# A state space layer in two halves of channels: the first half's tables, inputs and scan inside the input projection

## The reference: what is computed

```python
u = rmsnorm(x, g_mix[1]) @ w_in_c                # 2048 -> 1024 channels
# 64 groups of 16 channels, 64 complex states each
xr, xi = einsum('btgc,gpc->btgp', u, bb_re), einsum('btgc,gpc->btgp', u, bb_im)
xr[:, 0] += ar * s0_re - ai * s0_im              # the past state enters at the first token
sr, si = complex_scan(ar, ai, xr, xi)            # s[t] = a * s[t-1] + x[t], complex, per state
y = einsum('btgp,gcp->btgc', sr, c_re) - einsum('btgp,gcp->btgc', si, c_im) + d_skip * u
y = gelu(y)
mix = (y @ w_glu_v) * sigmoid(y @ w_glu_g)
```

## Time and profile before

| | us |
|---|---|
| median of 3 runs | 2754.16 |
| lowest and highest | 2751.86, 2755.89 |
| the profiled execution | 2755.66 |
| its span in the profile | 2753.1 |
| TensorE busy | 2707.5 (98%) |
| VectorE busy | 1592.7 (58%) |
| ScalarE busy | 1168.8 (42%) |
| GpSimd busy | 445.2 (16%) |

### The profile page before, as it was taken

How to read it: one execution, slowest core, us unless ns; L and a number is a source line. 1 busy time by engine, 2 the same in 40 slices (tenths; PEclk the granted TensorE clock), 3 DMA queues, 4 the chain that set the end, 5 groups by cost and what they waited for, 6 DMA issues and landing times.

```text
span 2753.1 us, 54151 instructions
## 1 busy us (share of the span) xinstructions
PE 2707.5 (98%) x19993; PEld 2676.2 (97%) x19993; DVE 1592.7 (58%) x2615; ACT 1168.8 (42%) x1514; POOL 445.2 (16%) x535
## 2 busy tenths in 40 slices
PE   8999999999999999999999998999999999999997
PEld 7999999999999999999999997999999999999997
DVE  7556666665554455655556657565554555455554
ACT  5554445434343343435554443544433344334333
POOL 1333333330000000070003561310000000000022
PEclk9999999999999999999999999999999999999998
DMA  6444444555545454444444531545555554555453
GB/s 176 133 132 132 135 144 127 147 150 152 144 141 143 143 145 140 135 141 143 143 133 141 145 94 46 150 142 148 150 145 153 147 151 139 152 154 152 143 145 93
DMA packets 739213, 382.97 MB, mean 139 GB/s; under 512 B 13560, under 2 KB 734756, under 8 KB 739140
## 3 DMA queue, kind: packets, MB, share of 16 engines
q1 hardware_dynamic: 722352, 365.34, 46.4%
q10 hardware_dynamic: 14228, 9.31, 1.1%
q0 software_dynamic: 2560, 7.29, 1.0%
HBM read 373.31 MB, written 8.57 MB: 139 GB/s over the span
## 4 chain that ended last, share of the span: by engine, by line
PE 96%; DVE 2%; ACT 1%; issue 0%; DMA 0%; ACTq 0%; SPq 0%; POOL 0%; POOLq 0%; DVEq 0%
PE banks L1591 31%; PE banks L1592 30%; PE banks L1593 30%; PE banks L1656 1%; PE banks L1974 0%; PE banks L2026 0%; PE banks L1871 0%; DVE wl L1032 0%; DMA xin<-in_x_sample 0%; DVE m L1472 0%; DVE m L1470 0%; PE banks L1961 0%; PE banks L1754 0%; PE banks L1652 0%; PE banks L1752 0%
## 5 line engine op out<-in xcount | busy, mean ns | idle before, releaser
L1032 DVE TENSOR_TENSOR wl<-raw,wh 128x1024 fp32r<-128x1024 f32 x708 | 897.0, 1268 | 802.1 <-ACT wh L486 801.3
L1591 PE MATMUL banks<-h,wh 128*128 128x336 f32 (+2 forms) x3648 | 1157.5, 317 | 3.9 <-DVE wl L1078 2.2
L486 ACT ACTIVATE wh<-raw 128x1024 fp32r<-128x1024 f32 x708 | 748.8, 1058 | 949.6 <-PE banks L1593 932.0
L1592 PE MATMUL banks<-h,wh 128*128 128x336 f32 (+2 forms) x3648 | 1146.4, 314 | 0.0
L1593 PE MATMUL banks<-h,wl 128*128 128x336 f32 (+2 forms) x3648 | 1145.0, 314 | 0.0
L1591 PEld LDWEIGHTS banks<-h,wh 128*128 128x128 f32 x3648 | 686.3, 188 | 11.7 <-issue 7.9
L1592 PEld LDWEIGHTS banks<-h,wh 128*128 128x128 f32 x3648 | 686.2, 188 | 1.7
L1593 PEld LDWEIGHTS banks<-h,wl 128*128 128x128 f32 x3648 | 685.5, 188 | 0.0
L1591 PE MATMUL banks<-act,wh 128*128 128x336 f32 (+2 forms) x1872 | 588.1, 314 | 2.7 <-DVE act L1546 2.1
L1592 PE MATMUL banks<-act,wh 128*128 128x336 f32 (+2 forms) x1872 | 585.9, 313 | 0.0
L1593 PE MATMUL banks<-act,wl 128*128 128x336 f32 (+2 forms) x1872 | 585.6, 313 | 0.0
(11 more groups left out here) (370 smaller groups left out, 1700.0 us busy)
## 6 DMA issues: line engine op xcount, KB each, us to landing
raw<-in_w_up SPq DMA_DIRECT2D x172, 512.0 KB, 3.8
raw<-in_w_gate SPq DMA_DIRECT2D x172, 512.0 KB, 3.8
raw<-in_w_down SPq DMA_DIRECT2D x160, 448.0 KB, 3.6
raw<-in_w_in_e SPq DMA_DIRECT2D x96, 512.0 KB, 3.7
raw<-in_w_out_e SPq DMA_DIRECT2D x32, 512.0 KB, 4.0
raw<-in_w_down SPq DMA_DIRECT2D x32, 512.0 KB, 4.0
raw<-in_w_in_c SPq DMA_DIRECT2D x16, 512.0 KB, 3.7
raw<-in_w_glu_v SPq DMA_DIRECT2D x16, 512.0 KB, 4.0
```

The lines of the kernel that those rows point to most:

```text
L486: sc.activation(wh[:, j % RING, :], raw[:, j % RING, :], ACT.Copy).then_inc(rounded, 1)
L1032: v.tensor_tensor(wl[:, j % RING, :], raw[:, j % RING, :], wh[:, j % RING, :].bitcast(F32), ALU.subtract) \
L1591: pe.matmul(out, whi, hi, start=first and k == 0, stop=False)
L1592: pe.matmul(out, whi, lo, start=False, stop=False)
```

## The change

The state space's 8 chunks are treated as two halves of four. Each of the four tables is made, turned and copied once for either half (`TURNED`: eight half tables, the first four for chunks 0 to 3). `BX`, `BT` and the scan's scratch `m0`, `m1` have half the size; the second half's `BT` lies where the first half's was. The states lie in two tensors, `xsA` and `xsB`. TensorE makes input chunks 0 to 3 in the middle and behind tiles (2, 0) and (2, 1), always in banks 4 to 7; chunk 4 directly behind the projection, chunks 5 to 7 after `K5`. ScalarE takes chunks 0 to 3 at the places of `X_TAKEN`. VectorE scans quarters 0 and 1 behind the splits of tiles (2, 1) to (3, 1) (`SCANNED`), quarters 2 and 3 one by one after the projection. The direct path's table is summed in bank 2, its skip is added behind the split of (3, 3) instead of (3, 2). The third readout table goes to a plain `C3` on GpSimd, and ScalarE spreads both `C3` and `C4` into block form. GpSimd copies past states once per half. ScalarE copies the first half's block ends into `SC`. In the diff, lines that only remove the old form are partly left out.

```diff
-BX_TURNED = [(0, 3), (1, 3), (2, 2), (3, 1)]
-BX_COPIED = [(1, 0), (2, 0), (2, 3), (3, 2)]
+TURNED = {(0, 2): 0, (0, 3): 1, (1, 1): 2, (1, 3): 3, (2, 2): 4, (2, 3): 5, (3, 1): 6, (3, 2): 7}
+FOUR_PAIRS = PAIRS // 2
+SCANNED = {(2, 1): ((0, 1),), (2, 2): ((0, 2), (0, 3)), (3, 0): ((1, 1), (1, 2)), (3, 1): ((1, 3),)}
+X_TAKEN = {(1, 3): (0,), (2, 0): (1, 2), (2, 1): (3,)}
...
+        BT, BX, m0, m1 = union(
+            0, ("BT", [P, 4, STEP, 2, P]), ("BX", [P, 2, 4, P]), ("m0", [P, 2, QUARTER * BLK]), ("m1", [P, 2, QUARTER * BLK]),
+            )
+        xsA, st5 = union(16 * slot_bytes - 4 * NS * 2 * PAIRS - 4 * 2 * FOUR_PAIRS * XW, ("xsA", [P, 2, FOUR_PAIRS, XW]), ("st5", [P, NS, 2, PAIRS]))
+        C3, = union(4 * 4 * STEP * 2 * P, ("C3", [P, 2, PAIRS, C5]))
...
+        SCt, = union(8 * slot_bytes, ("SCt", [P, 2, PAIRS, PCH]))
+        g0, g1 = union(0, ("g0", [P, 2, 3, 4, PAIRS]), ("g1", [P, 2, 3, 4, PAIRS]))
...
-        CT3 = BX.rearrange("p r j n -> p (r j) n").rearrange("p (j r) n -> p j r n", r=2)
...
+        xsB, CT3, CT4, SC, fin5 = union(at_h, ("xsB", [P, 2, FOUR_PAIRS, XW]), ("CT3", [P, 8, 2, P]), ("CT4", [P, 8, 2, P]),
+                                        ("SC", [P, PCH, 2, PAIRS]), ("fin5", [P, 1 + NS, 2, PAIRS]))
+        halves5 = (xsA, xsB)
...
-            src = wide[(j + 1) % 2]
-            dst = xs[:, :, 4 * j:4 * j + 4, :].rearrange("p r q x -> p q r x")
+            src = wide[1 if j < 4 else (j + 1) % 2]
+            dst = halves5[j // 4][:, :, j % 4 * 4:j % 4 * 4 + 4, :].rearrange("p r q x -> p q r x")
...
+                    if (i, j) in TURNED:
+                        k = TURNED[i, j]
+                        for r in range(2):
+                            e.wait_ge(bt_t, 2 * k + r + 1)
+                            sc.activation(BT[:, :, k % STEP, r, :], bank[4 + k % 2 * 2 + r].rearrange("p (j n) -> p j n", j=4),
                                           ACT.Copy).then_inc(bt_c, 1)
+                    for m in X_TAKEN.get((i, j), ()):
+                        e.wait_ge(x5, m + 1)
+                        take_x(lambda to, x: sc.activation(to, x, ACT.Copy), m).then_inc(x5a, 1)
...
-            for j in range(8):
+            for j in range(4, 8):
...
+            for n, (to, src, ready) in enumerate(((CT3, C3, c3_made), (CT4, C4, c4_made))):
+                e.wait_ge(ready, 1)
+                e.wait_ge(ct_zero, n + 1)
+                for g in range(2):
+                    rowsl = slice(g * P5, (g + 1) * P5)
+                    for r in range(2):
+                        ins = sc.activation(to[rowsl, :, r, :].rearrange("p j (q g c) -> p j q g c", q=4, g=2)[:, :, :, g, :],
+                                            src[rowsl, r].rearrange("p (j q) c -> p j q c", q=4), ACT.Copy)
+                ins.then_inc(ct34_made, 1)
+            e.wait_ge(scan5, 2)
+            sc.activation(SC[:, :, :, 0:FOUR_PAIRS].rearrange("p c r q -> p r q c"), xsA[:, :, :, 3 * BLK:3 * BLK + PCH], ACT.Copy).then_inc(sc_a, 1)
...
+            past = lambda x, n: gp.tensor_copy(x[:, :, :, BLK + PCH:2 * BLK],
+                                               st5[:, :, :, n * FOUR_PAIRS:(n + 1) * FOUR_PAIRS].rearrange("p s r q -> p r q s"))
+            past(xsA, 0).then_inc(st_a, 1)
             st.then(gp.memset(BX[:], 0.0))
...
+            half = lambda t: t[:, 0:FOUR_PAIRS]
+            other = lambda t: t[:, FOUR_PAIRS:PAIRS]
+            for n in range(2 * STEP):
+                k, j0 = n % STEP, 4 * (n // STEP)
+                own = slice(4 * j0, 4 * j0 + FOUR_PAIRS)
+                if k == 0:
+                    if n:
+                        e.wait_ge(bx_used, n)
+                    for g in range(2):
+                        rowsl = slice(g * P5, (g + 1) * P5)
+                        for r in range(2):
+                            to = BX[rowsl, r].rearrange("p j (q g c) -> p j q g c", q=4, g=2)[:, :, :, g, :]
+                            ins = gp.tensor_copy(to, B2[rowsl, r, own].rearrange("p (j q) c -> p j q c", q=4))
+                else:
+                    times_power(gp, st, B2, k - 1, 0, half(bp), half(bq), OF_B, j0, j0 + 4)
+                    gp.tensor_tensor(other(bp), B2[:, 1, own], power(k - 1, 1)[:, own], ALU.mult)
+                    st.then(gp.tensor_tensor(other(bq), B2[:, 0, own], power(k - 1, 2)[:, own], ALU.mult))
+                    e.wait_ge(bx_used, n)
+                    into_blocks(gp, half(bp), half(bq), BX[:, 0])
+                    ins = into_blocks(gp, other(bp), other(bq), BX[:, 1])
                 ins.then_inc(bx_made, 1)
-                e.wait_ge(bx_made, k + 1)
+                e.wait_ge(bx_made, n + 1)
...
-            e.wait_ge(bx_used, STEP)
...
+            e.wait_ge(bx_used, 2 * STEP)
+            for r in range(2):
+                for j0 in (0, 4):
+                    own = slice(4 * j0, 4 * j0 + FOUR_PAIRS)
+                    second = sq[:, 0:FOUR_PAIRS * C5].rearrange("p (q c) -> p q c", c=C5)
+                    times_power(gp, st, C0, 2, r, C3[:, r, own], second, OF_C, j0, j0 + 4)
+                    st.then(gp.tensor_tensor(C3[:, r, own], C3[:, r, own], second, ALU.add))
+            gp.memset(sq[:, 0:1], 0.0).then_inc(c3_made, 1)
             e.wait_ge(evac, PH["glu"].group(0, 0) + BANK_CREDIT)
-            gp.tensor_copy(xs[:, :, :, BLK + PCH:2 * BLK], st5.rearrange("p s r q -> p r q s")).then_inc(st_in, 1)
-            gp.memset(CT4[:], 0.0).then_inc(ct4_zero, 1)
+            past(xsB, 1).then_inc(st_in, 1)
+            for to in (CT3, CT4):
+                gp.memset(to[:], 0.0).then_inc(ct_zero, 1)
...
+            def scan_step(u, i):
+                q, xs = slice(u * QUARTER, (u + 1) * QUARTER), halves5[u // 2]
+                own = slice(u % 2 * QUARTER, (u % 2 + 1) * QUARTER)
+                if i == 1:
+                    e.wait_ge(x5a, 2 * u + 2)
+                    e.wait_ge(st_a, 1)
+                n = PCH if i == 1 else PCH + NS
+                prev, cur = (xs[:, :, own, BLK * k:BLK * k + n] for k in (i - 1, i))
+                A0 = AP5[:, 1:2, 3, q].unsqueeze(3).to_broadcast([P, 2, QUARTER, n])
+                A1 = AP5[:, 0::2, 3, q].unsqueeze(3).to_broadcast([P, 2, QUARTER, n])
+                m = lambda t: t[:, :, 0:QUARTER * n].rearrange("p r (q c) -> p r q c", c=n)
+                complex_step(m(m0), m(m1), A0, A1, prev)
+                if i < 3:
+                    st.then(v.tensor_tensor(cur, cur, m(m0), ALU.add))
+                elif u < 2:
+                    v.tensor_tensor(cur, cur, m(m0), ALU.add).then_inc(scan5, 1)
+                    e.wait_ge(scan5, u + 1)
...
+                    for u, k in SCANNED.get((i, j), ()):
+                        scan_step(u, k)
+                    if (i, j) == (3, 3):
+                        e.wait_ge(bx_used, 2 * STEP)
                         e.wait_ge(skip_made, 1)
-                        first = bank[6][:, 0:8 * C5].rearrange("p (j c) -> p j c", c=C5)
+                        first = bank[2][:, 0:8 * C5].rearrange("p (j c) -> p j c", c=C5)
...
-            scan_pairs(0, 1)
-            scan_pairs(1, 2)
-            scan_pairs(2, 4)
-
+            for u in (2, 3):
+                for k in range(1, 4):
+                    scan_step(u, k)
+            e.wait_ge(sc_a, 1)
...
-            def tables(k):
-
-                e.wait_ge(bx_made, k + 1)
-                if k:
-                    e.wait_ge(bt_c, 4 * k)
...
+            def tables(n):
+                k, j0 = n % STEP, 4 * (n // STEP)
+                e.wait_ge(bx_made, n + 1)
+                if n == 1:
+                    e.wait_ge(ms_inv, NORMS["win"] + 1)
+                if n >= 2:
+                    e.wait_ge(bt_c, 2 * n - 2)
+                if n == STEP:
+                    e.wait_ge(x5a, 4)
+                for r in range(2):
                     for m in range(4):
-                        ins = pe.transpose(bank[2 + b][:, m * P:(m + 1) * P], BX[:, b // 2, 4 * (b % 2) + m, :], ident[:])
+                        ins = pe.transpose(bank[4 + n % 2 * 2 + r][:, m * P:(m + 1) * P], BX[:, r, m, :], ident[:])
                     ins.then_inc(bt_t, 1)
-                for j in range(8):
+                for j in range(4):
                     for r in range(2):
                         for q in range(4):
-                            ins = pe.matmul(bank[6][32 * q:32 * q + 32, (8 * k + j) * C5:(8 * k + j + 1) * C5],
-                                            BX[:, r, j, 32 * q:32 * q + 32], C0[:, r, 4 * j + q, :], start=r == 0, stop=r == 1)
+                            at = (8 * k + j0 + j) * C5
+                            ins = pe.matmul(bank[2][32 * q:32 * q + 32, at:at + C5],
+                                            BX[:, r, j, 32 * q:32 * q + 32], C0[:, r, 4 * (j0 + j) + q, :], start=r == 0, stop=r == 1)
                 ins.then_inc(bx_used, 1)
+            def inputs(j):
+                to = wide[1 if j < 4 else (j + 1) % 2]
+                for r in range(2):
```

(64 more changed lines are left out.)

73 lines of the change are left out of this document (10 added, 63 removed).

## The result

The changed kernel takes 2762.19 us (median of 8 runs, 2759.08 to 2765.38) where the kernel before takes 2754.40 on the same chip (8 runs, 2751.15 to 2755.89): ratio 1.0030, 95% interval 1.0020 to 1.0041. It is slower by 7.8 us; the forecast was 2762.0. The profiled execution took 2760.78 us with a span of 2759.0.

The account below looks back on a forecast made before the run. TensorE is 98% busy, but VectorE's chain, started by GpSimd's past states, bounds the changed stage. Late scan +18.95 less 11.25 us of scan gives +7.7, 2763.4 for the profiled execution; adjusted towards the median, 2762; range 2750.5 to 2768.

Parts of the forecast that it names:

- The sum: First late scan (VectorE's first after the projection) starts 18.95 us later, less 11.25 us of scan taken away: +7.7 us.
- Stalls before half tables: In the input projection, TensorE waits for GpSimd's tables: 1.0 us before table 1, 1.4 before 5, 2.9 before 7.
- the price of a scan operation: GpSimd's delay per VectorE scan operation beside its tables: 0.28 or 0.42 us, bounded by 0 and whole length, 0.44 or 0.58.
- Inputs and tables on TensorE: In the projection, four input chunks add 7.6 us; eight half tables at 1.6 make 12.8 where there were 12.2.
- GpSimd behind it: After table 7: fourth readout table and skip until 1649.6, third table 7.4 us, past states 0.55, done at 1657.6.
- the walk: Step-by-step timing in trace clock from tables 0 to 3 through table 7, skip, input chunks and past states.
- VectorE: Late scan starts at 1657.7 instead of 1638.75; two quarters take 13.2 us, carries and first spread 16.3 unchanged.
- Who sets the end: Before the spread readout, VectorE's chain ends at 1687.2, TensorE at 1685.5; TensorE does not replace VectorE as limit.
- Rival 3: Every scan operation and split holds GpSimd up for its whole length, alternating strictly: +13.1 us, 2767.3; chance 0.15.

Follow-up runs that it names:

- Number 5: Changed kernel with SCANNED empty: quarters one and two scanned behind the input projection, ahead of the wait for past states; 2763.62 us, ratio 1.0041 to the kernel before.
- number 2: Changed kernel with fourth readout table and skip made by GpSimd before half table 5 instead of behind half table 7; 2757.05 us, ratio 1.0015 to the kernel before.
- numbers 2 to 4: Changed kernel with fourth readout table and skip earlier (1.0015); also quarters 0 and 1 scanned behind (2,0), (2,1) (1.0016); also K sooner (1.0006).
- numbers 7 and 8: Kernel before and changed kernel, both unchanged, each profiled a second time for TensorE's gaps; gated projection at 124.6 and 133.1 us.
- number 6: Changed kernel with earlier scans, fourth table and K, plus chunk 4 inside (3,3), first readout between convolutions and smaller moves; 2750.37 us, ratio 0.9993 to the kernel before.

## Why the prediction was right

The sum was +7.7; by the same chain the first pair of profiles shows +7.6 (first late scan 18.9 later, 11.2 less from there to the spread readout), and the medians +7.8. The path was right. That the sum is within 0.2 us is partly luck, for errors in its terms cancel. By its own steps:

- **Stalls before half tables**: 1.0, 1.4, 0, 2.9 forecast; 0.49, 0.71, 0, 1.30 measured. Here the price of a scan operation was too high. Number 5 gives it: without scans GpSimd is done with table 7 2.1 us sooner and with the skip 4.1 sooner, and has waited 0.85 for TensorE besides. For the sixteen operations beside the half tables that makes about 0.2 each, not 0.28 and 0.42; for the four beside the 512-column work of the fourth readout table about 0.5 each, more than the 0.42.
- **Inputs and tables on TensorE**: forecast 7.6 us for four chunks in the projection. From the start of table 3 to that of table 4 pass 21.5 us (1590.14 to 1611.67); less three tiles of 3.69 and a half table of 1.73 (a half table and its tile take 5.42) leaves 8.7. And eight half tables at 1.73 are 13.8, where I had 12.8. So 2.1 us too little here, 2.8 too much in the stalls; the end of (3,3) came out at 73.8 instead of 74.0 by two errors that cancel.
- **GpSimd behind it**: fourth table and skip 11.2 us (1633.96 to 1645.17), forecast 12.1. Third table and past states 9.1, forecast 8.0: I took all twelve operations at 0.62, but every third is an addition of 0.72, and they start 0.69 apart. Past states at 88.6, forecast 88.8: table 7 was 0.5 too late in the walk, this stretch 0.9 too long and the next 1.1 too short.
- **VectorE**: late scan at 88.6 (88.9), two quarters 13.19 (13.16), to the spread readout 16.30 (16.3). The wait before it shrank to 1.27 (1.6; the prediction's own times make it 1.7), in the second profile to 2.23. The clock was low for about half of chunks 5 to 7, much as for the first chunks in the first profile of before.
- **Who sets the end**: right for the change as made, and it is why number 2, a move of GpSimd work into its idle time, gives half of the loss back. TensorE was 1.3 to 2.2 us short of the limit, as the prediction had it (1.7). I did not carry that over: with the chain 6.8 us shorter the gated projection came only 4.7 sooner, and my forecasts for numbers 2 to 4, which followed VectorE's chain, came out 3 to 6 us too fast, each against the kernel before on the same chip.
- **Rival 3** took each operation as an exclusive hold. The Trainium skill, SBUF — State Buffer, section "Who interferes with whom", states such a lock. Number 5 speaks against it for these operations: twelve scan operations (4 of 272 columns, 8 of 400) that take 6.6 us alone took 10.6 (1642.71 to 1653.34), while GpSimd in the same stretch did ten that start 0.69 apart alone. Taken in turns these would need 6.6 + 6.9 = 13.5 us. They overlap in part, and both slow down, VectorE by 60% and GpSimd by 30%. For the split the page's rule stays near: GpSimd's 0.62 product took 1.48 to 1.71 beside it.

What was not tried: the half tables or the early inputs without the rest of the change. Their 2.1 us of work that I had not counted are read from traces alone.

## What to carry to other kernels

Work taken out of the middle of a chain counts only as far as what starts the chain stays where it is: here 11.25 us of scan left VectorE, and its first late operation came 18.9 later (88.6 instead of 69.7), because the engine that makes the tables had less room and the longer queue. Ask for each moved step which idle time of which engine it could have used; GpSimd had 17 us of it a few tiles earlier. And when a chain gets shorter, work out the second limit as closely as the first: here they were 1.3 to 2.2 us apart.

## What the runs showed of the hardware

TensorE's short matmuls seem to be bound by the arrival of their instructions. The gaps marked "issue" come after each 128 matmul and 128 weight load records, whatever is waited for. Two such stretches of number 2 (columns as above), and its DMA queue for instructions between 1663 and 1700 us:
```profile
1679.79:1683.68 3.89, 1.99 (x128) 1.83 (x129) 3.79 (x8) 2.31 (x9) 0.00 (x0) 1.00 0.01 4
1683.68:1687.57 3.89, 1.99 (x129) 1.83 (x129) 3.82 (x8) 2.00 (x8) 0.00 (x0) 1.00 0.01 4
```
```profile
q8 instruction: 9, 0.15, 1.4%
```
Nine packets of 0.15 MB together are 16 KB each, one about every 4 us, which is the period of the gaps (3.89). That their arrival is what ends a gap is inferred from this; no run changes it alone. 256 records thus cost 3.3 to 4.0 us, however short they are; work of 2.0 us leaves a gap of 1.2 to 1.9. The interval differs from one execution of a kernel to the next, and within one (numbers 7 and 8). The readouts (15 ns a record) run into it, the convolution (53 ns) does not, and mixing the two, as in number 6, shortens both together from 25.8 to 24.8 us at the same length of gap. The Trainium skill, Runtime: NRT & Kernel Launch, section "Instruction fetch mechanics", has engines refill 16 KiB blocks of 256 instructions, which agrees, but calls the cost mostly hidden; here it is not, with 1.2 to 1.9 us open per block. What sets its length within 3.3 to 4.0 us stays open.
